# Constant matmuls on TensorE ahead of five waits in the routing and the closing part of a diffusion backbone step

## The reference, cut to what matters

```
x  = LN1(alpha * x + gate1 * TokenMix(u))        # last step: merged rows @ w_out
u2 = x * (1 + scale2) + shift2
group  = top-1 of softmax(u2 @ w_r1 + b_r1)      # 4 groups
expert = top-2 of (u2 @ w_r2 + b_r2)[group]      # 4 experts in a group
hid    = silu(u2 @ w_up[e], first half) * (u2 @ w_up[e], second half)
y      = sum over the 2 chosen experts of e_w * (hid @ w_down[e])
x  = LN2(alpha * x + gate2 * y)                  # the last norm
```

## Time and profile before

| | us |
|---|---|
| median of three runs | 1034.57 (1033.0 to 1036.87) |
| the profiled execution, its own time | 1032.05 |
| its span from first to last instruction | 1030.2 |
| TensorE busy in it | 906.6 (88%) |
| mean granted TensorE clock | 0.939 of full speed |
| the routing part with four of the five waits | 645.83 to 688.26 |
| the fifth wait, before the closing sums | 982.72 to 993.83 |

### The profile page before, as it was taken

One profiled execution on the slowest core, in us unless ns is written; L12 is line 12 of the kernel. 1 busy time (PEld: TensorE's weight loads), 2 busy tenths in 40 slices (PEclk: granted clock), 3 DMA queues, 4 the chain that ended last, 5 costly groups with the idle time before them and its releaser, 6 DMA issues.

```text
span 1030.2 us, 22201 instructions
## 1 busy us (share of the span) xinstructions
PE 906.6 (88%) x8752; PEld 651.3 (63%) x8752; DVE 432.1 (42%) x861; ACT 335.7 (33%) x594; POOL 237.2 (23%) x306
## 2 busy tenths in 40 slices
PE   1799889999999999999999979359999999999953
PEld 0398668857777777776676767336656656665521
DVE  3634832004434454651324894642244341243318
ACT  1433302114434342431212210323345453254415
POOL 2276600000100000000000374212434433343340
PEclk9799988999999999998999979559999999999987
DMA  9978645332120301231012511996889999799552
GB/s 317 402 217 298 217 180 200 142 122 83 21 82 1 123 21 62 84 129 75 20 62 90 217 42 47 395 375 230 339 313 411 410 410 393 282 353 411 169 214 102
DMA packets 63946, 207.56 MB, mean 201 GB/s; under 512 B 7550, under 2 KB 7940, under 8 KB 60828
## 3 DMA queue, kind: packets, MB, share of 16 engines
q1 hardware_dynamic: 51536, 175.55, 45.1%
q0 software_dynamic: 8592, 26.39, 7.1%
q10 hardware_dynamic: 3772, 5.00, 1.5%
HBM read 186.96 MB, written 19.96 MB: 201 GB/s over the span
## 4 chain that ended last, share of the span: by engine, by line
PE 69%; DVE 12%; DMA 6%; ACT 6%; issue 3%; POOL 3%; SPq 1%; ACTq 0%; POOLq 0%; DVEq 0%
PE ps L1683 24%; PE ps L1941 15%; PE ps L1600 7%; PE ps L1926 6%; PE ps L1669 3%; DMA ring<-in_w_mod 2%; PE ps L1800 2%; PE ps L1916 2%; PE ps L1737 1%; ACT expert_w L1009 1%; DVE R_x L1224 1%; ACT w_hi L851 1%; POOL R_x L711 1%; PE ps L1973 1%; PE ps L1951 1%
## 5 line engine op out<-in xcount | busy, mean ns | idle before, releaser
L1941 PE MATMUL ps<-expert_w,R_p 128*32 128x256 f32 x3072 | 177.4, 383 | 0.9 <-ACT R_p L1032 0.7
L1941 PEld LDWEIGHTS ps<-expert_w,R_p 128*32 128x32 f32 x3072 | 100.0, 111 | 61.1 <-issue 3.9
L1683 PE MATMUL ps<-w_hi,uT_hi 128*128 128x512 f32 x320 | 134.7, 421 | 4.2 <-ACT R_x L948 2.4
L1683 PE MATMUL ps<-w_lo,uT_hi 128*128 128x512 f32 x320 | 127.8, 399 | 0.0
L1179 DVE TENSOR_TENSOR w_lo<-ring,w_hi 128x1024 fp32r<-128x1024 f32 x52 | 67.3, 1323 | 123.8 <-ACT w_hi L851 123.0
L1926 PE MATMUL ps<-expert_w,R_p 128*32 128x256 f32 x1536 | 91.7, 379 | 0.5 <-ACT R_p L1061 0.5
L1009 ACT COPY expert_w<-staged 128x1024 f32 (+1 forms) x87 | 85.5, 1044 | 19.8 <-PE ps L1941 8.6
L1517 DVE COPY expert_w<-staged 128x1024 f32 x105 | 69.7, 695 | 43.1 <-PE ps L1941 25.7
L1535 DVE TENSOR_TENSOR R_p<-R_p,ps 128x128 f32<-128x128 f32 x48 | 13.8, 287 | 151.6 <-ACT R_p L1051 151.6
L1683 PEld LDWEIGHTS ps<-w_hi,uT_hi 128*128 128x128 f32 x320 | 61.1, 191 | 21.1 <-issue 4.0
L1926 PEld LDWEIGHTS ps<-expert_w,R_p 128*32 128x32 f32 x1536 | 50.1, 110 | 33.3 <-ACT R_p L1061 0.8
(11 more groups left out here) (350 smaller groups left out, 1462.5 us busy)
## 6 DMA issues: line engine op xcount, KB each, us to landing
staged<-in_w_up SPq DMA_DIRECT2D x128, 512.0 KB, 12.1
staged<-in_w_down SPq DMA_DIRECT2D x64, 512.0 KB, 10.8
ring<-in_w_in SPq DMA_DIRECT2D x11, 2048.0 KB, 8.0
R_d<-in_w_mod SPq DMA_DIRECT2D x13, 1024.0 KB, 5.3
ring<-in_w_mod SPq DMA_DIRECT2D x8, 1024.0 KB, 20.5
y_slots<-R_s ACTq DMA_DIRECT2D x1, 4608.0 KB, 18.8
ring<-in_w_out SPq DMA_DIRECT2D x2, 2048.0 KB, 7.9
R_p<-in_w_mod SPq DMA_DIRECT2D x3, 1024.0 KB, 8.0
```

What stands on the lines that cost most here:

```text
L1683: i = mm(out, parts(k)[a][:, tok(j)], w[b][:, k], start=(k == 0 and a + b == 0), stop=(k == KD - 1 and b == 1))
L1941: m = mm(ps[SUB * g:SUB * (g + 1), 0, 0:256].rearrange("p (h n) -> p h n", h=2), xT[:, k % 4, at:at + SUB], up_w[:, k, :, P * g:P * (g + 1 ...
```

## The change: what it does

A helper `keep_busy(n)` is added to TensorE's list. It issues `n` fp32 matmuls of 128x512 with the identity matrix as stationary operand and the first 512 columns of the constants as moving operand, into PSUM bank 7. Nobody reads the result, and none of these matmuls waits for or raises a semaphore. It is called at five places: 6 before the last `route` (after a wait for the reader of tile 3's output product, so that bank 7 is free), 7 after it, 5 between `"rank"` and `"slots"`, 9 after `"slots"`, and 11 after the last down product.

```diff
+            def keep_busy(n):
+
+                for _ in range(n):
+                    mm(bank(7), ident, consts[:, 0:BW], start=True, stop=True)
+
             def route(j):
...
                 for jj in routed_after(j):
+                    if jj == NT - 1:
+                        was_read(pe, ("out", NT - 2))
+                        keep_busy(6)
                     route(jj)
+            keep_busy(7)
             pe.wait_ge(S["masks_ready"], 1)
             begin(pe, "rank")
...
             filled(i, "rank")
 
+            keep_busy(5)
             begin(pe, "slots")
...
             filled(i, "slots")
+            keep_busy(9)
...
             down_product(2 * last + 1)
+            keep_busy(11)
```

## The result

| | before | changed |
|---|---|---|
| median, 20 runs each | 1033.76 us (1031.38 to 1036.87) | 1027.92 us (1023.49 to 1032.97) |
| profiled execution | 1032.05 | 1026.46 |
| its span | 1030.2 | 1024.6 |
| mean granted TensorE clock | 0.939 | 0.966 |

The ratio of the times is 0.9944, 95% interval 0.9927 to 0.9960: 5.8 us less, where 4.9 were forecast (1029.7 us). The interval lies clear of no change; whether the gain reaches half a per cent it leaves open (0.40 to 0.73%).

A forecast was written before the change was run, and what follows sets the result against it. TensorE's waits and short pieces at 1.2 GHz, not its amount of work, were taken as the bound. Savings of 9.3 us less 4.4 losses left 4.9: 1034.57 to 1029.7 us, range 1025.3 less 0.3 to 1034.6.

The forecast's parts named there:

- the clock staying up throughout: Rival: the clock stays up through all five places, saving 9.3 us, time 1025.3 us; chance 0.22.
- the closing block alone: Rival: overruns cancel the routing and first up product savings, only closing sums gain 2.3 us, time 1032.3; chance 0.16.
- the slower one: Rival: the blocks of six and seven overrun at 1.2 GHz, together 8.7 us late, time 1041.0; chance 0.07.
- losses: Clock falls around the last routes and first gather cost 4.4 us: 2.5, 1.6, 0.3 and 0.
- Gap a: Route of tile 3, 3.6 us without dense work: a fall makes the six 1.0 late; at 0.3, cost 0.3 us.
- Gap b: After the six, idle plus route of tile 4, 5.2 us: a fall stretches the route and delays rank, cost 2.5.
- Gap d: After the five, through slots, 3.6 us: a fall costs the nine 2.4, hidden by their 3.1 us gather wait, so 0.
- Gap e: After the nine, first gather's landing and transposes, 4.8 us: a 0.65 fall slows the first up product, cost 1.6.
- The size of a fall: When dense work resumes, 3.9 to 5.6 us at 1.2 GHz lose 1.9 to 2.8 us; 2.4 taken.
- the load stream as free to move: Expert loop start: the weight stream nearly rests from 694 to 703 and moves along, so the loop keeps 7.0 us.
- The closing term: Closing sums: 24 records to the third tile's sum go from 12.46 to 10.1 us, saving 2.3.
- the signs that I had named: One or two short 1.2 GHz stretches between 650 and 690; wrong if blocks overrun above 2 us or sums start after 11.1.

The follow-up runs named there:

- routing blocks: The changed kernel without the 11 matmuls after the last down product, keeping those of 6, 7, 5 and 9: 1030.19 us, ratio 0.9960 to the kernel before.
- two gathers: The changed kernel with a separate buffer and index column for the first gather, the second issued right behind it: 1026.56 us, ratio 0.9934 to the kernel before.
- without the five: The changed kernel without the 5 matmuls between rank and slots: 1031.83 us, ratio 0.9982 to the kernel before.
- the block before tile 1's route: The changed kernel plus one wide product inside all five routes and five matmuls ahead of tile 1's route: 1024.35 us, ratio 0.9914 to the kernel before.

## Why the prediction was right, step by step

The forecast, with clock falls in some of the gaps and a gain of about 5 us, held; the pieces were nearly as worked out, the losses partly others. Of the rivals, the clock staying up throughout falls by the three stretches at 1.2 GHz, the closing block alone by the routing blocks' 0.9960 (0.9946 to 0.9974), and the slower one by the 0.9944 itself.

| step | forecast us | the two profiles us |
|---|---|---|
| 1 route of tile 4 | 2.5 | 6.30 to 3.78: 2.5 |
| 2 rank | 0.7 | 1.47 to 0.73: 0.7 |
| 3 slots | 0 | 4.44 to 2.39, hidden: 0 |
| 4 transposes | 1.0 | 1.94 to 1.08: 0.9 |
| 5 first up product | 2.8 | 6.41 to 3.66: 2.8 |
| 6 closing sums | 2.3 | 12.46 to 10.55: 1.9 |
| sum | 9.3 | 8.8 |
| losses | 4.4 | 2.3 |

The losses in the profile: the route starts 0.3 us after `u2` is ready, rank 0.8 after the masks, and the second gather is waited for 1.14. With these 8.8 - 2.3 = 6.5 us; the spans differ by 5.6, and the changed profile's last routes began 0.8 us later than those of before (642.87 against 642.05), for reasons ahead of the change. So the sum closes within 0.1.

That the total came so near is partly luck. With the falls as they were (1.1 us instead of 4.4) the working would have given 9.3 - 1.1 = 8.2 us, or 1026.4, below the forecast's 1027.5 to 1032.2; a wait that was overlooked (1.14) and a closing term that was too large (0.4) made up for much of the difference.

- *Gap a* had 0.3 of a fall; it fell (647.1), and the six were late by 0.3, not by the 1.0 taken for a whole fall. *Gap b*: it fell, but at 657.2, behind the route, so the route was not stretched at all, and the loss was 0.8 instead of 2.5. *Gap d*: a fall in the nine, absorbed as forecast. *Gap e*, with 0.65 of a fall and 1.6 us: none, since the nine, slowed in d, ran to 683.15 and left no gap. That falls follow each other through the blocks was not in my working.
- *The size of a fall* was the term that was mis-sized: I took 2.4 us from resumptions after long idle times (3.9 to 5.6 us at 1.2 GHz). With a block following at once the clock was down for 3.4 us each time in the changed profile, which costs half, 1.7.
- *What the steps left out* is the second gather. It is issued only after the first transposes and takes 6.23 us; the slow first up product had covered it before. I named the load stream as free to move and overlooked this transfer. The wait that took the place of the one removed cost 1.14 us here.
- *The closing term* was 0.4 too large: the third tile's sum takes 10.55 at 2.4 GHz, not 10.1, since the 36 records in 15.2 us include some that only reach into that stretch; over the whole of the changed closing sums it is 17.41 us for 40, 0.435 each.
- *The spread* of the changed kernel, 9.5 us over 20 runs against 5.5, fits falls that come at other places from one execution to the next: in the profile of the kernel with two gathers, whose TensorE list is the same up to there, the clock fell in the last route instead of behind it (and in that of the routing blocks alone in neither):

```profile
655.83 3.52 PE L1607 MATMUL ps<-router,R_p 128*128 128x20 f32 x16 [0.82 <-ACT R_p L1025]
659.18 8.01 PE L1864 MATMUL ps<-consts 128*128 128x512 f32 x14
```

That this makes the whole spread is argued, not shown: part of it arises ahead of the change, since in the ten profiles whose TensorE list is the same up to tile 3's route that route begins anywhere from 642.05 to 647.90 us.

Of the signs that I had named, three short stretches came instead of one or two, and no block was late by over 2 us. The closing sums did start a little later than 11.1 us after the last down product (11.2), but behind 1.54 us without work, so it was the gather and not the eleven that held them.

The Trainium skill, "TensorE: Matmul & The Clock Gate", section "A second HAM failure mode: psum-queue depth-cycling", had the clock swing between bursts; the profile agrees, with three falls after 640 us, but they cost 1.1 us on the path and not the 4.4 of my working.

## What to carry to other kernels

Where an engine other than TensorE sets the pace, look at how long TensorE's short pieces in the chain take, and whether they run at 1.2 GHz: work thrown away in the wait can halve them. Here it did so with products of 512 columns, in the routing part not with 16, and before the closing sums only where it reached near the end of the wait. Its length must be worked out at both clocks, because here an overrun was paid in full (5.9 us at rank, 6.5 at the last down product). And when a slow piece gets faster, look for the transfer that it had been covering.

## What was not expected of the hardware

With dense work following at once a fall lasted 3.4 us (three of three in the changed profile), though in the profile without the five 6.8 us (659.9 to 666.8) and then, over the slots and into the nine, 10.2 (677.0 to 687.2). Products of 16 columns kept TensorE busy for 40.65 of 47 us and did not bring the clock up. The indirect gather of 128 half rows took 6.2 to 6.4 us from issue to landing in the changed profile while the weight stream ran, and 7.6 for the second one in the profile with the block before tile 1's route.
